# Products of the 64 x 64 chunk matrices on four quarters of the TensorE array instead of the two diagonal ones

## What is computed

```python
def step(state, inp):
    r_t, w_t, k_t, v_t, kk_t, a_t = inp
    sa = jnp.einsum('bhvk,bhk->bhv', state, -kk_t)
    state = (state * w_t[:, :, None, :]
             + sa[..., None] * (kk_t * a_t)[:, :, None, :]
             + v_t[..., None] * k_t[:, :, None, :])
    return state, jnp.einsum('bhvk,bhk->bhv', state, r_t)
```

## Time and profile before

| | |
|---|---|
| median of three runs | 869.10 us |
| the profiled execution, its own time | 870.91 us |
| its span, first to last instruction | 869.1 us |
| TensorE matmul busy | 856.0 us, 98% of the span |
| VectorE / ScalarE / GpSimd busy | 541.8 / 394.6 / 6.8 us |
| mean share of the 16 DMA engines, bandwidth | 162 GB/s over the span |

### The profile page before, as it was taken

One profiled execution on the slowest core, in us unless ns is written; L12 is line 12 of the kernel. 1 busy time (PEld: TensorE's weight loads), 2 busy tenths in 40 slices (PEclk: granted clock), 3 DMA queues, 4 the chain that ended last, 5 costly groups with the idle time before them and its releaser, 6 DMA issues.

```text
span 869.1 us, 16493 instructions
## 1 busy us (share of the span) xinstructions
PE 856.0 (98%) x7230; PEld 790.6 (91%) x7230; DVE 541.8 (62%) x595; ACT 394.6 (45%) x464; POOL 6.8 (1%) x8
## 2 busy tenths in 40 slices
PE   9999999999999999999999999999999999999997
PEld 9999899998989999999999989988898899999996
DVE  5998754535777665555557655477654666655564
ACT  7552331356267544343447344456534544444332
POOL 0000110000000000000000000000000000000000
PEclk9999999999999999999999999999999999999999
DMA  9845412121474756555652744426353465555541
GB/s 296 281 140 193 146 51 99 51 98 51 167 253 137 243 158 219 173 176 192 194 193 98 242 146 146 146 98 225 130 179 97 130 209 193 184 177 185 187 140 49
DMA packets 96747, 140.62 MB, mean 162 GB/s; under 512 B 2480, under 2 KB 79408, under 8 KB 96688
## 3 DMA queue, kind: packets, MB, share of 16 engines
q1 hardware_dynamic: 96400, 139.62, 48.6%
q10 hardware_dynamic: 288, 0.13, 0.1%
HBM read 138.69 MB, written 1.05 MB: 161 GB/s over the span
## 4 chain that ended last, share of the span: by engine, by line
PE 93%; DVE 3%; ACT 2%; issue 1%; POOL 1%; POOLq 0%; DVEq 0%; ACTq 0%
PE PS L414 91%; ACT xh L1139 1%; DVE wlo L1553 1%; PE PS L519 1%; ACT whi L1139 1%; DVE xl L1584 0%; PE PS L974 0%; PE PS L643 0%; POOLq L97 0%; DVE xn L2099 0%; POOL TT L1128 0%; POOL TT L1132 0%; ACT junk L1139 0%; PE PS L1053 0%; DVE XT L1704 0%
## 5 line engine op out<-in xcount | busy, mean ns | idle before, releaser
L1553 DVE TENSOR_TENSOR wlo<-raw,whi 128x2048 fp32r<-128x2048 f32 x124 | 283.4, 2290 | 152.0 <-ACT whi L1139 151.9
L414 PE MATMUL PS<-xh,whi 128*128 128x256 f32 x1136 | 324.1, 287 | 3.3 <-DVE wlo L1553 2.0
L414 PE MATMUL PS<-xh,wlo 128*128 128x256 f32 x1136 | 320.7, 284 | 0.0
L414 PE MATMUL PS<-xl,whi 128*128 128x256 f32 x1136 | 317.0, 284 | 0.0
L1139 ACT ACTIVATE whi<-raw 128x2048 fp32r<-128x2048 f32 (+1 forms) x130 | 241.0, 1857 | 162.7 <-PE PS L414 162.4
L414 PEld LDWEIGHTS PS<-xh,whi 128*128 128x128 f32 x1136 | 218.4, 192 | 9.6 <-issue 3.5
L414 PEld LDWEIGHTS PS<-xh,wlo 128*128 128x128 f32 x1136 | 218.5, 192 | 0.0
L414 PEld LDWEIGHTS PS<-xl,whi 128*128 128x128 f32 x1136 | 216.2, 192 | 1.0
L414 PE MATMUL PS<-whi,fh 128*128 128x512 f32 x216 | 84.3, 391 | 0.0
L414 PE MATMUL PS<-wlo,fh 128*128 128x512 f32 x216 | 84.3, 390 | 0.0
L414 PE MATMUL PS<-whi,fl 128*128 128x512 f32 x216 | 84.0, 389 | 0.0
(11 more groups left out here) (305 smaller groups left out, 1086.2 us busy)
## 6 DMA issues: line engine op xcount, KB each, us to landing
raw<-in_w_in_dram SPq DMA_DIRECT2D x32, 1024.0 KB, 5.3
raw<-in_w_up_dram SPq DMA_DIRECT2D x16, 1024.0 KB, 5.3
raw<-in_w_down_dram SPq DMA_DIRECT2D x16, 1024.0 KB, 5.0
raw<-in_w_ffn_gate_dram SPq DMA_DIRECT2D x11, 1024.0 KB, 5.5
raw<-in_w_ffn_up_dram SPq DMA_DIRECT2D x11, 1024.0 KB, 5.3
raw<-in_w_ffn_down_dram SPq DMA_DIRECT2D x11, 1024.0 KB, 5.0
raw<-in_w_kv_mem_dram SPq DMA_DIRECT2D x8, 1024.0 KB, 5.4
raw<-in_w_o_dram SPq DMA_DIRECT2D x4, 1024.0 KB, 8.2
```

The lines of the kernel that those rows point to most:

```text
L414: return nc.tensor.matmul(o, l, r, start=start, stop=stop, **kw)
L1553: V.tensor_tensor(wlo[u % RING][:], raw[u % RING][:], whi[u % RING][:].bitcast(f32), ALU.subtract) \
```

## The change

The second token tile's transpose TT is put on the other half of the partitions, and so are Gm, AV, WT and a_tok. A product that reads XT, Tm or AK then writes to `half(c ^ tt)` (`out_of`), one that reads TT with Gm or AV writes back to `half(c)` (`back_to`); over the four pairs of chunk and tile both rotate through four quarters. The second half of `join` still reads and writes the same half. TT is no longer made by GpSimd out of XT but by a second `pairs` into banks 6 and 7 with a `pair_out` of its own. The four transposes of a_tok's second tile become eight plain products with the identity, one for each half of their columns. Ahead of the second tile's part of `join`'s second half, TensorE waits for the first half's products (semaphore joins). Counts of later semaphores move up by one.

```diff
-            def tokens(src, j0, done):
+            def tokens(src, j0, done, crossed=False):
                 for tt in range(NT):
                     for j in range(NPAIR):
+                        if crossed and tt == 1:
+                            for c in range(2):
+                                last = mm(PS[half(1 - c), (2 + tt) * 512 + j * P:(2 + tt) * 512 + (j + 1) * P],
+                                          src[:, j0 + j, P + c * CHUNK:P + (c + 1) * CHUNK], C("ident"), True, True)
+                            continue
                         last = nc.tensor.transpose(PS[:, (2 + tt) * 512 + j * P:(2 + tt) * 512 + (j + 1) * P],
                                                    src[:, j0 + j, tt * P:(tt + 1) * P], C("ident"))
...
-            def pairs(l, r, done, b=2):
+            def pairs(l, r, done, b=2, crossed=False):
...
-                            at0 = ((c ^ tt) * NPAIR + j) * HD
+                            at0 = ((c if crossed else c ^ tt) * NPAIR + j) * HD
+                            to = half(c ^ tt if crossed else c)
...
+            TURN = ((0, 0), (1, 1), (0, 1), (1, 0))
+            def out_of(lhs, rhs):
+                for s_ in range(NH):
+                    for c, tt in TURN:
+                        yield c, tt, s_, half(c ^ tt), 2 + c, lhs(c, tt, s_), rhs(c, tt, s_)
+            def back_to(lhs, rhs):
+                for s_ in range(NH):
+                    for c, tt in TURN:
+                        yield c, tt, s_, half(c), 2 + (c ^ tt), lhs(c, tt, s_), rhs(c, tt, s_)
             def lower(v):
                 pe.wait_ge(sem("t_ready"), v)
                 pe.wait_ge(sem("tt_ready"), v)
-                chunk_mms(HD, 0, lambda c, tt, x, s_: XT[half(c), x, s_, :], lambda c, tt, x, s_: Tm[half(c), x, s_, :], "g_mm")
+                for c, tt, s_, h, b, l, r in out_of(lambda c, tt, s_: XT[half(c), c ^ tt, s_, :], lambda c, tt, s_: Tm[half(c), c ^ tt, s_, :]):
+                    last = mm(PS[h, b * 512 + s_ * HD:b * 512 + (s_ + 1) * HD], l, r, True, True)
+                last.then_inc(sem("g_mm"), 1)
             def join(v):
                 pe.wait_ge(sem("g_ready"), v)
+                n = HD // 2
                 if v < 5:
-                    chunk_mms(HD // 2, 0, lambda c, tt, x, s_: TT[half(c), x, s_, :],
-                              lambda c, tt, x, s_: halves(Gm[half(c), x, s_, :], v, 0))
-                chunk_mms(HD // 2, 256, lambda c, tt, x, s_: Gm[half(c), x, s_, :],
-                          lambda c, tt, x, s_: halves(TT[half(c), x, s_, :], v, 1), "join_mm")
+                    for c, tt, s_, h, b, l, r in back_to(lambda c, tt, s_: TT[half(c ^ tt), c, s_, :],
+                                                         lambda c, tt, s_: halves(Gm[half(c ^ tt), c, s_, :], v, 0)):
+                        last = mm(PS[h, b * 512 + s_ * n:b * 512 + (s_ + 1) * n], l, r, True, True)
+                    last.then_inc(sem("joins"), 1)
+                for tt in range(NT):
+                    if tt == 1 and v < 5:
+                        pe.wait_ge(sem("joins"), v)
+                    for s_ in range(NH):
+                        for c in range(2):
+                            g = half(c ^ tt)
+                            o = (2 + c) * 512 + 256 + s_ * n
+                            last = mm(PS[g, o:o + n], Gm[g, c, s_, :], halves(TT[g, c, s_, :], v, 1), True, True)
+                last.then_inc(sem("join_mm"), 1)
...
                 if i == 1:
-                    pe.wait_ge(sem("pair_ready"), 2)
-                    tokens(eX, 0, "tok_T")
+                    pe.wait_ge(sem("pair_ready"), 3)
+                    tokens(eX, 0, "tok_T", True)
...
                     pairs(kk, eX, "pair_mm")
+                    pairs(kk, eX, "pair_mm", 6, True)
...
-            pool.wait_ge(sem("pair_ready"), 1)
-            nc.gpsimd.tensor_tensor(flat(TT), flat(XT), wide("above1"), ALU.mult).then_inc(sem("tt_masked"), 1)
             pool.wait_ge(sem("pair_ready"), 2)
+            nc.gpsimd.tensor_tensor(flat(TT), flat(TT), wide("eye"), ALU.add).then_inc(sem("tt_ready"), 1)
+            pool.wait_ge(sem("pair_ready"), 3)
             nc.gpsimd.tensor_tensor(flat(Tm), flat(Tm), wide("eye"), ALU.add).then_inc(sem("t_ready"), 1)
-            pool.wait_ge(sem("tt_masked"), 1)
-            nc.gpsimd.tensor_tensor(flat(TT), flat(TT), wide("eye"), ALU.add).then_inc(sem("tt_ready"), 1)
...
                 V.tensor_tensor(st2[:], st2[:], M("sb_neg").unsqueeze(1).broadcast_to([P, 2, 384]), ALU.mult).then_inc(sem("sb_lf"), 1)
+                if p_ == 0:
+                    pair_out(TT, "above1", 2, 6)
                 gate_unit(2 * p_)
```

More of the change, by code:

```diff
@@ L652, in pairs @@
                             ts = slice(tt * P + c * CHUNK, tt * P + (c + 1) * CHUNK)
-                            at0 = ((c ^ tt) * NPAIR + j) * HD
+                            at0 = ((c if crossed else c ^ tt) * NPAIR + j) * HD
+                            to = half(c ^ tt if crossed else c)
                             for e in range(2):
-                                last = mm(PS[half(c), (b + e) * 512 + at0:(b + e) * 512 + at0 + HD], l[half(e), j, ts],
+                                last = mm(PS[to, (b + e) * 512 + at0:(b + e) * 512 + at0 + HD], l[half(e), j, ts],
                                           r[half(e), j, ts], True, True)
                 last.then_inc(sem(done), 1)
[L659 to L668, removed]
+            TURN = ((0, 0), (1, 1), (0, 1), (1, 0))
[7 more added lines that the diff above has]
+                        yield c, tt, s_, half(c), 2 + (c ^ tt), lhs(c, tt, s_), rhs(c, tt, s_)
             def lower(v):
@@ L697, in before @@
                     pe.wait_ge(sem("tt_ready"), 3)
-                    pe.wait_ge(sem("pair_ready"), 3)
+                    pe.wait_ge(sem("pair_ready"), 4)
                     tokens(rw, 8, "tok_T")
@@ L705, in before @@
                             for c in range(2):
-                                o = (2 + c) * 512 + (tt * NPAIR + j) * HD
-                                last = mm(PS[half(e), o:o + HD], at_[half(c), tt, head(h)], TT[half(c), c ^ tt, slot(h), :], True, True)
+                                g = c ^ tt
+                                o = (2 + g) * 512 + (tt * NPAIR + j) * HD
+                                last = mm(PS[half(e), o:o + HD], at_[half(g), tt, head(h)], TT[half(g), c, slot(h), :], True, True)
                     last.then_inc(sem("chunk_mm"), 1)
@@ L728, in amid @@
                     pe.wait_ge(sem("chunk_ready"), 1)
-                    chunk_mms(HD, 0, lambda c, tt, x, s_: AK[half(c), x, s_, :],
-                              lambda c, tt, x, s_: vt_[half(c), tt, head(slot_head(s_))], "chunk_mm")
+                    for c, tt, s_, h, b, l, r in out_of(lambda c, tt, s_: AK[half(c), c ^ tt, s_, :],
+                                                        lambda c, tt, s_: vt_[half(c), tt, head(slot_head(s_))]):
+                        last = mm(PS[h, b * 512 + s_ * HD:b * 512 + (s_ + 1) * HD], l, r, True, True)
+                    last.then_inc(sem("chunk_mm"), 1)
                 else:
@@ L743, in behind @@
                     pe.wait_ge(sem("chunk_ready"), 2)
-                    chunk_mms(HD, 0, lambda c, tt, x, s_: TT[half(c), x, s_, :], lambda c, tt, x, s_: AV[half(c), x, s_, :], "chunk_mm")
+                    for c, tt, s_, h, b, l, r in back_to(lambda c, tt, s_: TT[half(c ^ tt), c, s_, :], lambda c, tt, s_: AV[half(c ^ tt), c, s_, :]):
+                        last = mm(PS[h, b * 512 + s_ * HD:b * 512 + (s_ + 1) * HD], l, r, True, True)
+                    last.then_inc(sem("chunk_mm"), 1)
                 else:
@@ L747, in behind @@
                     tokens(kk, 0, "tok_T")
-                    pe.wait_ge(sem("pair_ready"), 4)
+                    pe.wait_ge(sem("pair_ready"), 5)
                     pairs(kk, eP, "pair_mm", 4)
@@ L798, in state_part @@
                         o = e * 512 + j * HD
-                        last = mm(PS[half(c), o:o + HD], WT[half(e), c, tt, j, :], St[half(e), g, j, :], True, True)
+                        last = mm(PS[half(c), o:o + HD], WT[half(e), x, tt, j, :], St[half(e), g, j, :], True, True)
                 last.then_inc(sem("u_mm"), 1)
@@ L883, in _ @@
             state_part(1)
-            pe.wait_ge(sem("pair_ready"), 5)
+            pe.wait_ge(sem("pair_ready"), 6)
             y_values(0)
@@ L1738, in gate_unit @@
                 elif i == 7:
-                    pair_out(RK, "incl", 4, 4)
+                    pair_out(RK, "incl", 5, 4)
                 dve.wait_ge(sem("units_used"), U_G[i] + 1)
@@ L1742, in gate_unit @@
                 if i == 0:
-                    pair_out(Tm, "level1", 2)
+                    pair_out(Tm, "level1", 3)
                 elif i < 6:
@@ L1751, in _ @@
                 if p_ == 1:
-                    pair_out(AK, "strict", 3)
+                    pair_out(AK, "strict", 4)
                 dve.wait_ge(sem("sb_ln"), p_ + 1)
```

(2 more changed lines are left out.)

## The result

The changed kernel took 862.3 us, the median of five runs (861.24 to 864.13), against 869.14 for the kernel before in the same session: a ratio of 0.9915 with a 95% interval of 0.9901 to 0.9928. The forecast was 861.5 us, with a range of 859.7 to 863.7.

The account below looks back on a forecast made before the run. TensorE was taken as the bound. +0.1 up to `join(1)`, -2.1 for `lower` 2 to 5, -3.8 for four `back_to`, -1.8 for AK and AV: -7.6 from 869.1 gives 861.5 us, range 859.7 to 863.7.

Parts of the forecast that it names:

- up to `join(1)`: Units 0 and 1: all added costs, removed waits, the first lower's saving and its later level mask together give +0.1 us.
- `lower(3)`: Unit 3's lower run saves 0.92 us, but only 0.6 counts, because join then waits for DVE's level mask.
- `lower(4)`: Unit 4's lower run gains 0, as its level mask had only 0.08 us of margin before join.
- four `back_to` in `join`: Four runs in join go from two quarters to four, 1.88 to 0.94 us each, -3.8 us together.
- wait on joins: TensorE's wait amid join's second half, four times, costs 0 because earlier products cover it; bounds 0 and 0.6 us.
- Pace by quarters: TensorE takes one instruction in about 59 ns per quarter used: 29.5 ns on two quarters, 14.9 on four.
- lower bound taken: For back_to's new order, 14.9 ns an instruction was taken; the other bound, 25, was kept as a rival (chance 0.09, 864.7 us).
- 25-ns floor: Rival, chance 0.02: no TensorE instruction under 25 ns, so every run saves 0.28 instead of 0.92 us; 867.0 us.
- products held on their row half: Rival, chance 0.05: in back_to a row half's second product waits 0.22 us for the first to pass; +17.6, 879.1 us.
- The additions: Extra TensorE work: second pairs in unit 0, +0.94 us; a_tok 1.48 in place of 0.81, +0.67.
- The mask: DVE's level mask becomes late for join, so lower in units 2 to 5 saves 2.1 us in place of 3.7.
- The step that puts the transfers at nothing: No DMA is added or moved and the stage uses a quarter of the transfer rate, so transfers cost nothing.

Follow-up runs that it names:

- orders: The changed kernel with the same products of nine runs put in other orders over four, two or one quarters at a time; 871.98 us.
- mask_first: The changed kernel with DVE's level mask ahead of the weight tile's low part in each gate unit; 859.04 us, ratio 0.9880 to the kernel before.
- before_mask_first: The kernel before with DVE's level mask moved ahead of the weight tile's low part; 869.92 us against 869.22, ratio 1.0005.
- after_again: The changed kernel run again unedited, to see whether time follows the granted clock; 863.26 us, ratio 0.9922 to the kernel before.

## Why the prediction was right

| term of the sum | forecast, us | measured, us |
|---|---|---|
| up to `join(1)`: additions, waits gone, `lower(1)`, mask | +0.1 | -0.1 (16.97 to 16.89) |
| `lower(2)` up to its `join` | -0.92 | -0.92 (5.08 to 4.16) |
| `lower(3)` | -0.6 | -0.64 (5.08 to 4.44) |
| `lower(4)` | 0 | -0.01 (5.08 to 5.07) |
| `lower(5)` | -0.58 | -0.62 (5.08 to 4.46) |
| four `back_to` in `join` | -3.8 | -3.7 (1.88 to 0.95 each) |
| AK with the values | -0.92 | -0.92 (5.08 to 4.16) |
| TT with AV | -0.92 | -0.92 (2.01 to 1.09) |
| wait on joins, four times | 0 | 0 |
| torn run of eX with eN | not in the sum | +1.0 |
| together | -7.6 | -6.8 |

Point by point:

- *Pace by quarters.* Right, and shown by orders: 14.9 ns an instruction on four, whatever rotates with what. `back_to` in its new order lay at the lower bound taken. The rivals of a 25-ns floor and of products held on their row half had no place here: two column halves of one row half ran at 1.91 as the diagonal did. The 25 ns read from the earlier trace rows were no pace of their own: that run passes from one row half to the other, and so holds a change of quarters with its 0.17.
- *The additions.* The second `pairs` cost 0.94 (2.10 against 1.16); a_tok took 106.59 to 108.15, 1.56 against the 1.48 worked out from st with sv. L1757, now L1785, was at 0.96 and TensorE no longer waited for it.
- *The mask.* The margins read in the earlier trace rows gave each `lower`'s share to 0.04 us, and mask_first, with before_mask_first as its counterpart, shows the cause.
- *What failed.* The step that puts the transfers at nothing, as no DMA is added or moved and the stage uses a quarter of the transfer rate. That rate is a mean: from 115.26 to 119.03 one load holds the engines at a share of 0.89, and the instruction queue's packet goes only as it ends. The instructions that TensorE has read ahead are a margin like the mask's, which the faster products use up; the sum had no term for it, and it measured +1.0 us. No row of before shows a torn run.
- *The clock.* The forecast subtracted from a median and said nothing of half-clock stretches. The half-clock stretches move single runs by some 1.6 us each, more than the forecast's miss of 0.8, so a miss as small as that is partly luck: the medians differ by 6.8 us in the session of the result and by 7.4 in that of after_again (870.65 and 863.26). The test of the sum is the stage, 6.8 measured against 7.6.

The version to keep is mask_first: 1.2% below the kernel before, about 4 us below the change alone.

## What to carry to other kernels

For products of 64 x 64 count how many quarters of the array a run rotates through, not how busy TensorE looks: at the full granted clock the pace here was one float32 instruction in about 59 ns for each quarter, whatever the order and for 32 and 64 columns alike. When a step gets faster, measure the margin of what is due right behind it on the other engines, each unit by itself; two instructions that changed places on DVE were worth 1.5 us, a fifth of the whole change. And a faster instruction stream must be read as well: look at the instruction queue's packets beside the large loads.

## What the runs showed of the hardware that was not expected

- A run that passes on to quarters that were idle saves 0.17 us at the change (1.91 against 2.08 for the same 64 instructions).
- An instruction packet of 16 KB moved only as a 1 MB load ended (118.85 us, the load issued at 114.23), and TensorE lost 1.0 us. With the load held back it went at 117.0.
- The granted clock fell to half in the middle of a kernel whose TensorE is at 98% over the span, once 2.6 us behind a wait of 0.83 us among short products (157.7 us); the cause stays open.
